# Prompt attention of a decoder layer: one more unit in flight, scores in two PSUM banks, each branch turned through its own

## The reference

```
s_s = einsum(q, ks) * scale + bias;  p_s = masked_softmax(s_s, d_s >= 0);  o_s = einsum(p_s, vs)
s_w = einsum(q, kw) * scale + bias;  p_w = masked_softmax(s_w, ...);       o_w = einsum(p_w, vw)
o = g[0] * o_c + g[1] * o_s + g[2] * o_w
```

## Time and profile before

| | |
|---|---|
| median of 3 runs | 1267.23 us (1264.92 to 1268.16) |
| the profiled execution | 1266.38 us, its span 1264.4 us |
| PE, DVE, ACT, POOL busy | 1221.5, 801.0, 572.5, 193.9 us |
| instructions | 25031 |
| the stage of the change | 646.11 (first turn) to 728.1 us (last values) |

### The profile page before, as it was taken

How to read it: one execution, slowest core, us unless ns; L and a number is a source line. 1 busy time by engine, 2 the same in 40 slices (tenths; PEclk the granted TensorE clock), 3 DMA queues, 4 the chain that set the end, 5 groups by cost and what they waited for, 6 DMA issues and landing times.

```text
span 1264.4 us, 25031 instructions
## 1 busy us (share of the span) xinstructions
PE 1221.5 (97%) x9304; PEld 1091.1 (86%) x9304; DVE 801.0 (63%) x1460; ACT 572.5 (45%) x1015; POOL 193.9 (15%) x379
## 2 busy tenths in 40 slices
PE   5999999999999999999988998999999999999997
PEld 3899999999999999997555667999999999978775
DVE  1787877742333366242587766588988888733466
ACT  2365555532221135343466655146555666523443
POOL 3000000000000036552292061031000000041000
PEclk9999999999999999999999999989999999999999
DMA  9935555556332335768242063633333233394563
GB/s 294 276 104 182 161 179 169 173 172 211 126 116 77 89 103 120 165 169 257 70 126 60 2 201 110 208 102 101 101 93 99 85 91 99 97 296 131 156 191 127
DMA packets 222195, 179.88 MB, mean 142 GB/s; under 512 B 48136, under 2 KB 199480, under 8 KB 222025
## 3 DMA queue, kind: packets, MB, share of 16 engines
q1 hardware_dynamic: 215201, 160.28, 43.2%
q0 software_dynamic: 6896, 18.35, 4.9%
HBM read 169.47 MB, written 13.35 MB: 145 GB/s over the span
## 4 chain that ended last, share of the span: by engine, by line
PE 86%; DVE 6%; ACT 4%; issue 1%; DMA 1%; DVEq 1%; SPq 0%; POOL 0%; ACTq 0%; POOLq 0%
PE ps L1500 30%; PE ps L367 26%; PE ps L1101 11%; PE ps L326 3%; PE ps L2990 2%; ACT AR L2378 2%; PE ps L1656 2%; PE ps L2978 1%; PE ps L2165 1%; PE ps L309 1%; PE ps L1708 1%; DVE AR L2548 1%; PE ps L2274 1%; PE ps L2182 1%; PE ps L447 1%
## 5 line engine op out<-in xcount | busy, mean ns | idle before, releaser
L1500 PE MATMUL ps<-UH,WH 128*128 128x288 f32 x512 | 152.2, 297 | 0.9 <-DVE RS L1588 0.9
L1500 PE MATMUL ps<-UH,WL 128*128 128x288 f32 x512 | 150.9, 295 | 0.0
L1500 PE MATMUL ps<-UL,WH 128*128 128x288 f32 x512 | 150.6, 294 | 0.0
L286 DVE TENSOR_TENSOR WL<-RAW,WH 128x1024 fp32r<-128x1024 f32 x61 | 76.2, 1250 | 114.6 <-ACT WH L282 112.5
L1500 PE MATMUL ps<-TB,WH 128*128 128x288 f32 x736 | 148.7, 294 | 0.0
L282 ACT ACTIVATE WH<-RAW 128x1024 fp32r<-128x1024 f32 x61 | 64.3, 1056 | 143.0 <-PE ps L367 128.6
L1500 PEld LDWEIGHTS ps<-TB,WH 128*128 128x128 f32 x736 | 118.1, 188 | 0.0
L1448 DVE TENSOR_TENSOR WL<-RAW,WH 128x512 fp32r<-128x512 f32 x144 | 99.1, 688 | 28.5 <-ACT WH L1443 28.4
L1500 PE MATMUL ps<-TB,WL 128*128 128x288 f32 x368 | 108.7, 295 | 0.0
L367 PE MATMUL ps<-UH,WH 128*128 128x288 f32 x480 | 103.9, 297 | 1.6 <-DVE WL L286 1.6
L1443 ACT ACTIVATE WH<-RAW 128x512 fp32r<-128x512 f32 x144 | 90.3, 627 | 29.0 <-PE ps L1500 24.2
(11 more groups left out here) (459 smaller groups left out, 2724.6 us busy)
## 6 DMA issues: line engine op xcount, KB each, us to landing
AW<-in_w_ada_dram SPq DMA_DIRECT2D x42, 512.0 KB, 4.5
RAW<-in_w_ffn_in_dram SPq DMA_DIRECT2D x72, 256.0 KB, 3.0
RAW<-in_w_ffn_out_dram SPq DMA_DIRECT2D x36, 512.0 KB, 3.8
RAW<-in_w_ffn_in_dram SPq DMA_DIRECT2D x34, 512.0 KB, 3.9
AR<-in_w_ffn_in_dram SPq DMA_DIRECT2D x18, 512.0 KB, 3.9
AR<-in_w_ada_dram SPq DMA_DIRECT2D x7, 1024.0 KB, 11.4
RAW<-in_w_ffn_out_dram SPq DMA_DIRECT2D x16, 448.0 KB, 3.8
AR<-in_w_ada_dram SPq DMA_DIRECT2D x14, 512.0 KB, 6.1
```

Of the source, the lines that this page charges most:

```text
L286: nc.vector.tensor_tensor(WL[:, slot, :], RAW[:, slot, :], WH[:, slot, :].bitcast(F32), ALU.subtract).then_inc(split_done, 1)
L1500: mm = nc.tensor.matmul(acc(bank), W[g % 4][:, k * P:(k + 1) * P], R[:, k, :], start=(k == 0 and z == 0 and i in (0, 1, 3)), stop=(k == HK ...
```

## The change

A third set of four X tiles (`XSETS` = 3), two of them in the space of `FACX`, two in an unused part of `K1`. The scores of both branches go into banks 0 and 1, so branch 1 of a unit waits for branch 0's tiles to be biased, and branch 0 for branch 1 of the unit before. Branch 0 is turned through banks 4 and 5, branch 1 through 2 and 3 (`TBANK`). The order on the engines changes: TensorE computes the scores of unit u+1 before it turns unit u-1, VectorE biases unit u+1 where it biased unit u, and ScalarE does the exponentials of unit u before it evacuates unit u-1.

```diff
+        XS2 = sb("XS2", [P, HK * HT])          # over the space of FACX
...
             def scores(u, br):
...
-                    if u:
-                        pe.wait_ge(x_ready, 4 * (u - 1) + i + 1)
-                    nc.tensor.matmul(ps[:, i, 0:n], ...
+                    if u or br:
+                        pe.wait_ge(x_ready, 4 * u + i - 1)
+                    nc.tensor.matmul(ps[:, g, 0:n], ...
             def turn(u, br):
-                if u or br:
-                    pt_wait(pe, *((u, 0) if br else (u - 1, 1)))
+                if u:
+                    pt_wait(pe, u - 1, br)
...
-                        mm = nc.tensor.transpose(ps[:, 4 + g, ...
+                        mm = nc.tensor.transpose(ps[:, TBANK[br] + g, ...
...
             scores(0, 0)
-            pe.wait_ge(cmp_d, CPT_READ)
             scores(0, 1)
...
             for u in range(NU + 1):
+                if u + 1 < NU:
+                    scores(u + 1, 0)
+                if u > 1:
+                    values(u - 2, 1)
+                if u + 1 < NU:
+                    scores(u + 1, 1)
                 if u == 1:
                     pe.wait_ge(vc_ready, 1)
+                    pe.wait_ge(cmp_d, CPT_READ)
                 if u:
                     turn(u - 1, 0)
-                if u > 1:
-                    values(u - 2, 1)
-                if u:
                     turn(u - 1, 1)
-                if u + 1 < NU:
-                    scores(u + 1, 0)
-                    scores(u + 1, 1)
-                if u:
                     values(u - 1, 0)
                 sample_cmp_pe(pe, u - 1)
...
             for u in range(NU + 1):            # ScalarE
+                if 0 < u < NU:
+                    exps(u)
+                if u % 4 == 1 and u > 1:
+                    o_evac(act, u // 4 - 1)
                 if u:
                     pt_evac(act, u - 1, 0)
-                if u % 4 == 1 and u > 1:
-                    o_evac(act, u // 4 - 1)
-                if 0 < u < NU:
-                    exps(u)
-                if u:
                     pt_evac(act, u - 1, 1)
...
             def biased(u, i):
-                if u >= 2:
-                    dve.wait_ge(t_done, 2 * (u - 2) + i // 2 + 1)
-                elif u == 1:
+                if u >= XSETS:
+                    dve.wait_ge(t_done, 2 * (u - XSETS) + i // 2 + 1)
+                elif u == 2:
                     dve.wait_ge(natp_out, 32)
...
+            for i in range(4):                 # VectorE
+                biased(0, i)
             for u in range(NU + 1):
                 if u:
                     weighted(u - 1)
-                if u < NU:
+                if u + 1 < NU:
                     for i in range(4):
-                        biased(u, i)
+                        biased(u + 1, i)
                 if u:
                     pt_evac(dve, u - 1, 1)
                 sample_cmp_dve(dve, u - 1)
...
-        X = [v[:, q * 512:(q + 1) * 512] for v in (v4["X"], v1["X2"]) for q in range(4)]
+        XSETS, TBANK = 3, (4, 2)
+        X = [v[:, q * 512:(q + 1) * 512] for v, n in ((v4["X"], 4), (XS2[:, :], 2), (v1["K1"][:, 3072:4096], 2), (v1["X2"], 4))
+             for q in range(n)]
```

More of the change, by code:

```diff
@@ L157, in build @@
         STT = sb("STT", [TT, 9 * NT])
-        FACX = sb("FACX", [P, HK * HT], F32R)
+        over_f = ExitStack()
+        FACX = sb("FACX", [P, HK * HT], F32R, over_f)
+        over_f.close()
+        XS2 = sb("XS2", [P, HK * HT])
         ADS = RS[:, 0:2 * ACOL]
@@ L2152, in scores @@
                     i = 2 * br + g
-                    if u:
-                        pe.wait_ge(x_ready, 4 * (u - 1) + i + 1)
-                    nc.tensor.matmul(ps[:, i, 0:n], QT[64 * g:64 * g + 64, 4 + r, t * P:(t + 1) * P],
+                    if u or br:
+                        pe.wait_ge(x_ready, 4 * u + i - 1)
+                    nc.tensor.matmul(ps[:, g, 0:n], QT[64 * g:64 * g + 64, 4 + r, t * P:(t + 1) * P],
                                      QT[64 * g:64 * g + 64, (MKS, MKW)[br], 0:n], start=True, stop=True).then_inc(s_mm, 1)
@@ L2164, in turn @@
                     for k in range(t + 1):
-                        mm = nc.tensor.transpose(ps[:, 4 + g, k * P:(k + 1) * P], X[xslot(u, 2 * br + g)][:, k * P:(k + 1) * P],
+                        mm = nc.tensor.transpose(ps[:, TBANK[br] + g, k * P:(k + 1) * P], X[xslot(u, 2 * br + g)][:, k * P:(k + 1) * P],
                                                  IDN[:, :])
@@ L2527, in biased @@
                 dve.wait_ge(s_mm, 4 * u + i + 1)
-                if u >= 2:
-                    dve.wait_ge(t_done, 2 * (u - 2) + i // 2 + 1)
-                elif u == 1:
+                if u >= XSETS:
+                    dve.wait_ge(t_done, 2 * (u - XSETS) + i // 2 + 1)
+                elif u == 2:
                     dve.wait_ge(natp_out, 32)
-                nc.vector.tensor_tensor_reduce(out=X[k][:, 0:n], in0=ps[:, i, 0:n], in1=GS[:, r + REP * (i % 2), (t + 1) * P - 1::-1],
+                nc.vector.tensor_tensor_reduce(out=X[k][:, 0:n], in0=ps[:, i % 2, 0:n], in1=GS[:, r + REP * (i % 2), (t + 1) * P - 1::-1],
                                                scale=1.0, scalar=TOP, op0=ALU.add, op1=ALU.min,
@@ L2691, in build @@
         VNW = AWF.rearrange("p (b c n) -> p b c n", b=NB, c=2)
-        NMX, SUM, WGT = MU[:, 0:8], MU[:, 16:24], MU[:, 32:40]
+        NMX, SUM, WGT = MU[:, 0:12], MU[:, 16:28], MU[:, 32:44]
         NM8 = MU[:, 48:80].rearrange("p (h t) -> p h t", h=NH)
@@ L2922, in xslot @@
         def xslot(u, i):
-            return 4 * (u % 2) + i
+            return 4 * (u % XSETS) + i
         def pt_on_act(u, br):
@@ L2942, in pt_evac @@
             if eng is nc.scalar:
-                nc.scalar.activation(PT[br][:, :, 0:n], ps[:, 4:6, 0:n], ACT.Copy).then_inc(pt_a, 1)
+                nc.scalar.activation(PT[br][:, :, 0:n], ps[:, TBANK[br]:TBANK[br] + 2, 0:n], ACT.Copy).then_inc(pt_a, 1)
             else:
-                nc.vector.tensor_copy(PT[br][:, :, 0:n], ps[:, 4:6, 0:n]).then_inc(pt_d, 1)
+                nc.vector.tensor_copy(PT[br][:, :, 0:n], ps[:, TBANK[br]:TBANK[br] + 2, 0:n]).then_inc(pt_d, 1)
         def o_evac(act, r):
```

## The result

The changed kernel takes 1281.09 us (median of 4 runs, 1277.88 to 1284.47) where the kernel before takes 1267.68 beside it: a ratio of 1.011 with an interval of 1.009 to 1.0129. It is slower by some 14 us, where the forecast had 5.2 and its range ended 3.6 us lower. Medians are of all executions, and the ratios leave out two with a far lower mean granted clock: 1422.17 us at 0.82, one of the four of "The banks alone, without the longer flight", and 1979.04 us at 0.56, one of the ten of the second version in "Can the filling be shortened?".

The account below looks back on a forecast made before the run. The prediction took the order of work in prompt attention, not any engine, to bound its cycles. Profiled 1266.38 plus 3.6 for the stage and 1.6 for the clock gave 1271.6, or 1272.4 against the runs' median; range 1262.5 to 1277.5.

Parts of the forecast that it names:

- The exponentials leave the path: Prompt attention: exponentials finish before VectorE asks, removing 8.0 us of waits; separate branch banks remove most of TensorE's 8.8 us.
- The other side's rival: Prompt-attention cycles: exponentials decide, not the gate; cycle 17.7 us, total about 1261, decided by a cycle under 18.9; chance 0.17.
- The rival in which the change does not do what it says: ScalarE: exponentials still end late behind evacuations, adding waits of 2 us a cycle; total 1280, chance 0.05.
- the filling costs less: Stage start: VectorE weights early units between GpSimd's instructions, so 3 us come back; total about 1268, chance 0.22.
- Two score banks put a gate in their place: Branch 1's scores wait for VectorE's first two biased sums, with turns queued behind; a cycle 20.24 us, 20.8 and 22.35 with decode.
- the score matmul's duration in the chain from gate to gate: TensorE's score matmul, first term of each gate step: 0.48, 0.39, 0.27, 0.16 us at n=4, 3, 2, 1.
- n(u-1)=2: Gate-to-gate step where the turned unit has size 2: 4.68 us before decode steps.
- n=4: Gate-to-gate step where the turned unit has size 4, ScalarE evacuates and TensorE is last: 5.47 us.
- n=3: Gate-to-gate step where the turned unit has size 3: 5.72 us before additions.
- The clock: TensorE's idle gap in the filling makes the granted clock fall: +1.6 us, bounds 0 and 1.6.
- The filling: Stage start gets longer: unit 0 turned at 651.7 instead of 646.11, 5.6 us late.
- The emptying gets shorter: Stage end, exponentials done ahead: unit 12 turns 7.0 us late, but last values come at 731.7 against 728.1, +3.6 us.

Follow-up runs that it names:

- The banks alone, without the longer flight: Kernel before with two score banks and separate turn banks for each branch, its order and two sets of X tiles kept: 1351.19 us, 1.0674.
- the second version in "Can the filling be shortened?": Changed kernel with four score banks, unit 1's scores ahead of the 17 small matmuls, 10 and 8 unused transposes around the first turn: 1266.12 us, 1.0002.
- The runs at full clock: Changed kernel with unused transposes filling TensorE's gaps, 1277.25 us, 1.0075; the same idea with the first turn ahead of the gated scores, 1273.78 us, 1.0051.
- the first version under "Keeping TensorE busy": Changed kernel with unused transposes ahead of the gated scores, 24 for unit 2 and 6 for most later units: 1276.61 us, 1.0076.
- the second version, with a few dozen unused transposes more: Changed kernel with 24 unused transposes ahead of unit 2's gated scores, 8 at later gates, 6 after each scores of unit 1: 1277.25 us, 1.0075.

## Why the prediction was right in its sign and wrong in its size

*The exponentials leave the path: right.* The 8.0 us are gone, and so are the 8.8 us that weight loads waited between the branches. The other side's rival, by which this would have decided, fell with its condition: it wanted cycles under 18.9, and they took 24.0 and 24.8. The rival in which the change does not do what it says came near in its number, 1280, and fell by its mechanism, waits for exponentials. That the filling costs less fell too: it costs more. The other side's sum was wrong in itself: it names waits of 1.3 and 2.5 us, 3.8 together, and takes only 2.5 off the cycle; with both it would be 16.4 instead of 17.7. And about 1268 for the filling that costs less leaves out the clock's 1.6.

*Two score banks put a gate in their place: right, and shown.* With four banks the loss is gone (1.011 to 0.9998). TensorE waits before score matmuls, released by biased sums, and VectorE idles before the evacuation of branch 1 (0.96 us at size 3; I had 1.5).

*The term that failed is the score matmul's duration in the chain from gate to gate*: 0.48 at n=4 down to 0.16 at n=1, "a quarter" of the records. It measures 1.16 us until VectorE sees it at size 4, and a gated pair takes 1.73, 1.39, 1.04 and 0.49 us for n = 4 to 1. The trace of the kernel before had it in a row that the prediction did not use, a pair of size 4 (TensorE in order of time):

```profile
639.05 1.13 PE L2155 MATMUL ps<-AR 64*128 64x512 f32 x4
```

So the turns behind the gate come later than in the sum, and VectorE is without work between its pairs of biased sums, which the sum had back to back. Every step from gate to gate came out longer, by 0.2 to 0.6 us:

- n(u-1)=2 took 5.49 and 5.76 us where the sum had, decode steps included, 5.01 and 5.27. In the step shown above the excess is the first term: 1.11 us from the open gate to the turn, against 0.48 and the 0.14 for signals. Turns, evacuation, weighting and sums together are right to 0.01.
- n=4 is to be read at full clock, from 729.14 to the gated pair at 734.87: 5.73 us, where the sum to that point has 5.31. Here too it is the first term, 0.68 until the turn at 729.82 against 0.27.
- n=3, from the start of a gated pair of size 1 to the next open gate, took 6.42 and 6.19 us where the sum with TensorE's small pieces has 6.08 and 5.98.
- n=1 took 4.95 and 6.2 against 4.37 and 5.79. I have not taken these and those at n=3 apart.

The Trainium skill says that matmuls in different row groups of the array execute at the same time (TensorE: Matmul & The Clock Gate, "Packing small matmuls — row/col tiling"). The trace agrees, with 1.13 us for a pair let go together and 1.73 for one let go in turn, and the prediction should have read its group of four with it.

*The clock: the mechanism right, its count wrong.* I had one fall, in the filling, at 1.6 us. It fell there (0.50 from 654 to 656), after 4 us in which TensorE was busy for 0.35 and 0.43 of 2 us each. This agrees with what the Trainium skill (TensorE: Matmul & The Clock Gate, "HAM oscillation") says of a TensorE left idle between bursts. It fell twice more. Ahead of the second fall TensorE was busy for 1.07 us from 672 to 674 and 1.63 from 674 to 676, ahead of the third for 1.75 and 1.84 from 700 to 704; why it fell there, the third time above all, stays open. The size-4 step, from the open gate to the next gated pair, took 7.12 and 7.13 us instead of 5.73, so 1.4 more each, in the score pair and the turn that run at half the clock.

*The filling: too short by 2.2 us.* Unit 0's first transpose came at 655.06, or 653.9 less the 1.1 us of the later start, against 651.7. A sum of unit 1 waited 2.36 us for its score, and the weighting of unit 0 began at 649.52, or 648.4, where the sum had 647.0. From the open gate to the turn it then took 1.2 us at the lower clock, where the sum had 0.27. GpSimd's contention was rightly counted for unit 0: its four products took 3.16 us, where the sum had 1.67 + 1.5.

*The emptying gets shorter: right*, 13.92 against 13.4 us for the last stretch.

So the 10.9 us between +3.6 and +14.5 are by stretch: filling 2.2, then 2.5, 3.2 and 2.4 for the cycles, and 0.6 for the emptying. With its 1.6 for one fall the forecast had 5.2, and 9.3 are to be explained: two more falls are 2.8 of them, and by difference 6.5 are the scores' duration, 0.4 at each of 15 gates. The eight steps of the two middle cycles, read as above and those at n=4 at full clock, are over by 0.2 to 0.6 each and by 3.3 us in all, which is the same 0.4. The runs at full clock agree: 9 to 10 us of loss are left, of which some 3 come from the turn queued behind the gate. How much the clock alone costs stays open between the 4 us that filling TensorE's holes gave back and some 2 more that the added transposes may have cost.

## What to carry to other kernels

When a buffer is shared, the time of its producer enters the chain as latency, from the start of the instruction to the moment its reader sees it; a group's time over its count gives only the rate, and the two differ most where instructions run side by side. A gate costs its own length and everything that stands behind it in an engine's queue: of 14 us here, some 3 at full clock, and 6 to 8 together with the falls of the clock that went with them, were a turn that needed nothing of what the gate waited for. And where a change has two parts that lean on each other, price each alone: the longer flight was worth nothing in the median, the banks cost some 85 us. Before you compare two medians, look at the mean granted clock of each execution: it can differ within one kernel.

## What the runs showed of the hardware

**Side by side by row halves.** Two fp32 matmuls of 64 rows and 512 columns on different halves of the rows take 1.13 us together; with one started 0.6 us after the other the pair takes 1.73.

**The clock fell on a busy TensorE.** In the kept trace of the first version under "Keeping TensorE busy", TensorE was busy for 9.49 of the 10 us from 690 to 700, and for all of the last 2, at a clock of 1.00; from 700 to 702 the clock was 0.59. The stretches of the earlier trace rows, of which the first has TensorE busy for 19.96 of 23.89 us, stayed at 1.00. In the second version, with a few dozen unused transposes more, TensorE was busy for 9.50 us from 690 to 700 and the clock stayed at 1.00 throughout. I have no rule that parts these.

**Executions of one kernel differ in the clock.** Of 20 executions of the kernel before, timed beside "The banks alone", ten with a mean granted clock of 0.989 or more took 1265.3 us in the mean, and ten below it 1268.5.

**Products beside GpSimd.** Four products of VectorE, 1.67 us alone, took 3.16 us beside GpSimd. The Trainium skill (SBUF — State Buffer, "SBUF: two separate sides") describes the port that the two share as locked for a whole instruction by whichever comes first, for some forms of VectorE's instructions; the trace agrees as far as these products took nearly twice as long beside GpSimd.
